# A new order for the head of a hybrid layer: x first, modulation in five groups, seven column units

## What is computed

```python
def reference(x, c, ...):
    c_act = silu(c)
    mod = c_act @ w_mod + b_mod                 # 1024 -> 6 * 1024
    sh_m, sc_m, gt_m, sh_f, sc_f, gt_f = split(mod, 6)
    h = rms_norm(x, g_pre_mix) * (1.0 + sc_m) + sh_m
    y = hybrid_mixer(h, w_in, ...)
    x = x + gt_m * rms_norm(y, g_post_mix)
    h = rms_norm(x, g_pre_mlp) * (1.0 + sc_f) + sh_f
    y = square(relu(h @ w_up)) @ w_down
    return x + gt_f * rms_norm(y, g_post_mlp)

def hybrid_mixer(h, ...):
    b_a, c_a, v_a, x_b, g_b, u_a, u_b = split(h @ w_in, 7)
    y_a = b_a * causal_dwconv(c_a * v_a, conv_a_w, conv_a_b)     # 3 taps
    x_b = causal_dwconv(x_b, conv_b_w, conv_b_b)                 # 4 taps
    r = sigmoid(block_diag(x_b, w_r) + b_r)                      # 8 blocks of 128
    i = sigmoid(block_diag(x_b, w_i) + b_i)
    a = exp(-8 * r * softplus(-lam))
    rec = linear_scan(a, sqrt(1 - a * a) * (i * x_b))
    y_b = rec * gelu(g_b)
    m = sigmoid(u_a) * (y_a @ w_a_out) + sigmoid(u_b) * (y_b @ w_b_out)
    return m @ w_o
```

## Time and profile before

| | |
|---|---|
| Time, median of 3 runs | 849.9 us (848.84 to 850.04) |
| Span of the profiled execution | 846.6 us, from its first to its last instruction |
| Between the span and the median | 3.3 us |
| TensorE matmuls busy | 819.2 us, 97% |
| VectorE | 459.7 us, 54% |
| ScalarE | 379.5 us, 45% |
| GpSimd | 19.8 us, 2% |
| Chain that ended last | TensorE 93%, VectorE 4%, ScalarE 1%, transfers 1% |
| Transfers | 109.42 MB, mean 129 GB/s |

### The profile page before, as it was taken

How to read it: one execution, slowest core, us unless ns; L and a number is a source line. 1 busy time by engine, 2 the same in 40 slices (tenths; PEclk the granted TensorE clock), 3 DMA queues, 4 the chain that set the end, 5 groups by cost and what they waited for, 6 DMA issues and landing times.

```text
span 846.6 us, 10887 instructions
## 1 busy us (share of the span) xinstructions
PE 819.2 (97%) x3714; PEld 682.4 (81%) x3714; DVE 459.7 (54%) x598; ACT 379.5 (45%) x530; POOL 19.8 (2%) x21
## 2 busy tenths in 40 slices
PE   3699999999999999999999999999999999999997
PEld 3578888888888888888888898888888888888885
DVE  5966776666676556555774664333333433333335
ACT  6337777666665444444343653222222322222233
POOL 2311000000000000000000000000000000000000
PEclk9699999999999999999999999999999999999999
DMA  9934333325068666666337034333332223233202
GB/s 306 316 107 107 106 105 105 105 81 180 25 190 237 180 188 197 198 194 178 124 125 224 14 87 125 99 99 99 99 99 90 89 95 100 99 99 99 99 0 99
DMA packets 136438, 109.42 MB, mean 129 GB/s; under 512 B 3925, under 2 KB 120801, under 8 KB 136417
## 3 DMA queue, kind: packets, MB, share of 16 engines
q1 hardware_dynamic: 136192, 109.10, 42.9%
q0 software_dynamic: 160, 0.04, 0.0%
q10 hardware_dynamic: 64, 0.02, 0.0%
HBM read 107.04 MB, written 2.10 MB: 129 GB/s over the span
## 4 chain that ended last, share of the span: by engine, by line
PE 93%; DVE 4%; ACT 1%; DMA 1%; issue 1%; SPq 0%; DVEq 0%; ACTq 0%
PE ps L330 31%; PE ps L331 31%; PE ps L332 31%; DVE mod L837 3%; DMA xs<-in_x_dram 1%; ACT junk L506 1%; PE ps L1265 0%; PE ps L1165 0%; DVE ht_lo L883 0%; DVE k_pos L818 0%; PE ps L1238 0%; PE ps L1237 0%; ACT xnt L531 0%; ACT ht_hi L533 0%; DVE xnt L859 0%
## 5 line engine op out<-in xcount | busy, mean ns | idle before, releaser
L788 DVE TENSOR_TENSOR w_lo<-raw,w_hi 128x1024 fp32r<-128x1024 f32 x131 | 160.2, 1224 | 63.4 <-ACT w_hi L493 56.7
L330 PE MATMUL ps<-ht_hi,w_hi 128*128 128x512 f32 x448 | 177.0, 395 | 3.0 <-DVE ht_lo L883 3.0
L331 PE MATMUL ps<-ht_lo,w_hi 128*128 128x512 f32 x448 | 176.5, 394 | 0.0
L332 PE MATMUL ps<-ht_hi,w_lo 128*128 128x512 f32 x448 | 176.0, 393 | 0.0
L493 ACT ACTIVATE w_hi<-raw 128x1024 fp32r<-128x1024 f32 x132 | 138.3, 1050 | 37.6 <-PE ps L332 31.2
L330 PE MATMUL ps<-h_hi,w_hi 128*128 128x512 f32 (+1 forms) x288 | 105.5, 366 | 0.0
L331 PE MATMUL ps<-h_lo,w_hi 128*128 128x512 f32 (+1 forms) x288 | 105.4, 366 | 0.0
L332 PE MATMUL ps<-h_hi,w_lo 128*128 128x512 f32 (+1 forms) x288 | 105.4, 366 | 0.0
L330 PEld LDWEIGHTS ps<-ht_hi,w_hi 128*128 128x128 f32 x448 | 85.3, 190 | 20.7 <-issue 3.0
L332 PEld LDWEIGHTS ps<-ht_hi,w_lo 128*128 128x128 f32 x448 | 85.3, 190 | 18.0
L330 PE MATMUL ps<-w_hi,hd_hi 128*128 128x512 f32 x256 | 99.7, 390 | 0.0
(11 more groups left out here) (181 smaller groups left out, 1012.3 us busy)
## 6 DMA issues: line engine op xcount, KB each, us to landing
raw<-in_w_in_dram SPq DMA_DIRECT2D x52, 512.0 KB, 4.8
modraw<-in_w_mod_dram SPq DMA_DIRECT2D x32, 512.0 KB, 4.2
raw<-in_w_mlp_up_dram SPq DMA_DIRECT2D x32, 512.0 KB, 4.1
raw<-in_w_mlp_down_dram SPq DMA_DIRECT2D x32, 512.0 KB, 3.3
mod_raw<-in_w_mod_dram SPq DMA_DIRECT2D x16, 512.0 KB, 6.6
xs<-in_x_dram SPq DMA_DIRECT2D x8, 512.0 KB, 6.3
raw<-in_w_a_out_dram SPq DMA_DIRECT2D x8, 512.0 KB, 5.3
raw<-in_w_b_out_dram SPq DMA_DIRECT2D x8, 512.0 KB, 5.7
```

The lines of the kernel that those rows point to most:

```text
L330: nc.tensor.matmul(dst, l_hi, r_hi, start=first, stop=False)
L331: nc.tensor.matmul(dst, l_hi, r_lo, start=False, stop=False)
L332: return nc.tensor.matmul(dst, l_lo, r_hi, start=False, stop=last)
L788: V.tensor_tensor(w_lo[:, slot, :], raw[:, slot, :], f(w_hi[:, slot, :]), ALU.subtract).then_inc(w_lo_ready, 1)
```

## The change

What it does:

- SyncE loads x first. The vectors follow the second tile of x. Then the modulation and the first weights alternate.
- The modulation comes in five groups of channel blocks, (0), (1), (2, 3), (4, 5), (6, 7). Its pieces are 16 chunks of 512 KB (two transfers of 256 KB each), in 8 buffers instead of 3 larger ones. Group 0 is summed by TensorE alone, from the raw chunks, with c_act as the moving operand; the others by VectorE as before, group 1 with 2 x 128 columns to a step.
- Seven column units are summed block by block instead of five: the three first and the three second of XB, C and V, with B of n = 1. The weights come as one transfer of 512 KB to each channel block, with 256 columns of each of B, C, V and XB (those of n = 0 and 1). B of n = 0 (unit 7) is split from the same load and done as a column unit of its own.
- w0_hi and w0_lo are rings of four channel blocks, 896 columns each. w0_lo is made by VectorE, not by GpSimd.
- The softplus steps stand behind the head, not between the steps on mod0.
- TensorE then does unit 7, gates(0), units 8 and 9, gates(1), units 10 and 11, and the loop begins at n = 3. PSUM banks of n = 0 and 1 and of the first gates change; c_sb and the product C x V of n = 1 stand ahead of its convolution.

The diff, cut to its core:

```diff
+    GROUPS = ((0,), (1,), (2, 3), (4, 5), (6, 7))
+    N_FIRST, W0_RING = 7, 4
...
+        FIRST_BANK = ((0, 1, 2, 7), (6, 4, 5, 3))
+        FIRST_DONE = ((1, 2, 3, 8), (4, 5, 6, 7))
+        FIRST_UNITS = ((0, 5, 0), (1, 1, 0), (2, 3, 0), (0, 6, 1), (1, 2, 1), (2, 4, 1), (3, 0, 1))
...
+            def load_mod0(c):
+                g, m, num = CHUNKS[c]
+                if c >= M0_BUFS:
+                    g0, m0, num0 = CHUNKS[c - M0_BUFS]
+                    if g0 == 0:
+                        sp_eng.wait_ge(mod0_sum, 1)
+                    else:
+                        sp_eng.wait_ge(mod0_acc, acc_count(g0, m0 + num0 - 1))
+                ks = GROUPS[g]
                 for a in range(2):
+                    sp_eng.dma_start(chunk_view(c)[:, :, a, :],
+                                     w_mod_v[:, m:m + num, a * D + ks[0] * P:a * D + (ks[-1] + 1) * P]).then_inc(mod0_in[c % M0_BUFS], 16)
...
+            def load_first_units(g):
+                for k in GROUPS[g]:
+                    src = w_in_v[:, k, 0:4 * D].rearrange("p (j n) -> p j n", j=4)
+                    sp_eng.dma_start(raw0[:, k, :].rearrange("p (j n) -> p j n", j=4),
+                                     src[:, :, 0:2 * P]).then_inc(raw0_in[g], 16)
...
-            load_mod0(0)
             for t in range(TB):
                 sp_eng.dma_start(xs[:, t, :], x_v[:, t, :]).then_inc(xr_in[t], 16)
-                if t == 0:
+                if t == 1:
                     load_vectors(sp_eng, vectors[1::3], vec_in)
...
+            load_mod0_group(0)
+            load_first_units(0)
+            load_first_units(1)
+            load_mod0_group(1)
+            load_first_units(2)
+            load_mod0_group(2)
+            load_first_units(3)
+            load_mod0_group(3)
+            load_mod0_group(4)
+            load_first_units(4)
...
-            for q in range(NB // 2):
-                pool.wait_ge(w0_hi_ready, q + 1)
-                nc.gpsimd.tensor_tensor(w0_lo[:, :, cs], raw0[:, :, cs], w0_hi[:, :, cs].bitcast(f32),
-                                        ALU.subtract).then_inc(w0_lo_ready, 1)
...
+            act.wait_ge(xnt_ready, 4)
+            modulate(0, 0)
+            first_units_hi(1)
+            act.wait_ge(xnt_ready_dve, 4)
+            modulate(1, 1)
+            for g in (2, 3):
+                first_units_hi(g)
+                for k in GROUPS[g]:
+                    modulate(k, g)
+            modulate(6, 4)
+            first_units_hi(4)
+            modulate(7, 4)
+            A(w_hi[:, 3, :].rearrange("p (k n) -> p k n", k=NB), raw0[:, :, 0:P], ACT.Copy).then_inc(w_hi_ready, 1)
+            split_hi(2 * RING, 0)
+            act.wait_ge(sp_step, 1)
+            A(sp[:, 1, :], sp[:, 0, :], ACT.Exp).then_inc(sp_act, 1)
...
+            first_units_lo(0)
+            modulation_columns(0)
+            input_lo(0)
+            first_units_lo(1)
+            accumulate(1, range(NB))
+            modulation_columns(1)
+            accumulate(2, range(0, 2))
+            input_lo(1)
+            accumulate(2, range(2, NB))
+            first_units_lo(2)
+            modulation_columns(2)
+            accumulate(3, range(0, 2))
+            input_lo(2)
+            accumulate(3, range(2, 4))
+            input_lo(3)
+            accumulate(3, range(4, NB))
+            first_units_lo(3)
+            modulation_columns(3)
+            accumulate(4, range(0, 2))
+            input_lo(4)
+            accumulate(4, range(2, 4))
+            input_lo(5)
+            accumulate(4, range(4, NB))
+            modulation_columns(4)
+            input_lo(6)
+            first_units_lo(4)
+            input_lo(7)
...
+            split_lo(2 * RING, 0)
+            for i in range(SP_STEPS):
+                softplus_step(i)
...
-            mix(0, lambda: None, (RING + 2, RING + 3, RING + 4, None))
+            mix(0, lambda: None, (9, 10, 11, None))
             recurrence_gates(0)
-            mix(1, lambda: recurrence_scan(0), (None,) + tuple(2 * RING + j for j in range(1, RING)))
+            mix(1, lambda: recurrence_scan(0), (None,) * 4)
...
+            COLUMNS_AT = {(0, 3): 1, (1, 5): 2, (3, 1): 3, (5, 1): 4}
             for k in range(NB):
+                g = next(i for i, ks in enumerate(GROUPS) if k in ks)
+                pe.wait_ge(w0_lo_ready, g + 1)
                 pe.wait_ge(h_lo, k + 1)
+                for i, (j, col, n) in enumerate(FIRST_UNITS):
+                    if (k, i) in COLUMNS_AT:
+                        mod0_columns(COLUMNS_AT[k, i])
...
+            column_unit(N_FIRST, 3, ht_hi, ht_lo, bank(0, 3))
...
+            gates(0)
+            pe.wait_ge(xc_tap, 1)
+            column_unit(8, 0, ht_hi, ht_lo, 0)
+            pe.wait_ge(r_ready, 1)
+            column_unit(9, 1, ht_hi, ht_lo, 1)
+            gates(1)
+            pe.wait_ge(i_ready, 1)
+            column_unit(10, 2, ht_hi, ht_lo, 2)
+            pe.wait_ge(ya_f32, 2)
+            column_unit(11, 3, ht_hi, ht_lo, 3)
+            with pe.Fori(3, NB) as n:
+                mix(n)
```

More of the change, by code:

```diff
@@ L566, in recurrence_root, with mix @@
                 A(q_t[:, :], q_t[:, :], ACT.Sqrt).then_inc(mult_ready, 1)
-            def mix(n, after_xb, splits, xb_bank=0):
-                act.wait_ge(unit_done, 4 * n + 1)
+            def mix(n, after_xb, splits):
+                xb_bank = bank(n, 0)
+                act.wait_ge(unit_done, done(n, 0))
                 wait(act, xc_conv, 3 * n)
@@ L575, in mix @@
                   bias=cols[:, ds(C_BB + n, 1)]).then_inc(xc_tap, 1)
-                first = isinstance(n, int) and n == 0
+                first = isinstance(n, int)
                 if first:
-                    act.wait_ge(unit_done, 2)
-                    A(c_sb[:, :], ps[:, 1, :], ACT.Copy).then_inc(c_copied, 1)
+                    act.wait_ge(unit_done, done(n, 1))
+                    wait(act, cv_ready, n)
+                    A(c_sb[:, :], ps[:, bank(n, 1), :], ACT.Copy).then_inc(c_copied, 1)
                 if splits[0] is not None:
@@ L834, in mod0_steps @@
                         V.tensor_scalar(acc, part, c_act[:, 0:1], None, ALU.mult).then_inc(mod0_acc, 1)
                     else:
[L836 to L841 removed]
+                        dve.wait_ge(mod0_acc, acc_count(g, m - 1))
@@ new lines, in first_units_lo, with input_lo @@
+            def first_units_lo(g):
+                ks = GROUPS[g]
+                slot = ks[0] % W0_RING
+                dve.wait_ge(w0_hi_ready, g + 1)
+                V.tensor_tensor(w0_lo[:, slot:slot + len(ks), :], raw0[:, ks[0]:ks[-1] + 1, P:],
+                                f(w0_hi[:, slot:slot + len(ks), :]), ALU.subtract).then_inc(w0_lo_ready, 1)
+            def input_lo(k):
+                dve.wait_ge(h_hi, k + 1)
+                V.tensor_tensor(ht_lo[:, k, :], xnt[:, k, :], f(ht_hi[:, k, :]), ALU.subtract).then_inc(h_lo, 1)
@@ L914, in mix @@
             def mix(n, after_conv, splits):
-                first = isinstance(n, int) and n == 0
+                first = isinstance(n, int)
                 if first:
-                    dve.wait_ge(unit_done, 3)
-                    dve.wait_ge(c_copied, 1)
-                    V.tensor_tensor(cvp[:, KA - 1:], c_sb[:, :], ps[:, 2, :], ALU.mult).then_inc(cv_ready, 1)
+                    dve.wait_ge(unit_done, done(n, 2))
+                    dve.wait_ge(c_copied, n + 1)
+                    wait(dve, ca_conv, 2 * n)
+                    V.tensor_tensor(cvp[:, KA - 1:], c_sb[:, :], ps[:, bank(n, 2), :], ALU.mult).then_inc(cv_ready, 1)
                 dve.wait_ge(xc_tap, n + 1)
```

283 lines of the change are left out of this document (132 added, 151 removed).

## The result

The changed kernel takes 854.69 us (854.08 to 856.85, 4 runs) against 849.37 us (848.39 to 850.04, 4 runs) of the kernel before, measured together: a ratio of 1.0068, with a 95% interval from 1.0052 to 1.0083. It is 5.3 us slower, by more than a measurement can confuse with no change; the prediction was 849.2 us, with a range that ended at 852.2. The profiled execution of the changed kernel took 854.39 us, its span is 852.6 us: 6.0 more than before.

The account below looks back on a forecast made before the run. VectorE was taken to bound the head, transfers close behind, and matmuls the rest. The head's gain of 4.5 us less 3.8 of new wait gave -0.7: span 845.9, time 849.2 us; 8-in-10 range 845.6 to 852.2.

Parts of the forecast that it names:

- a new wait at gates(1): TensorE behind the head: two units no longer cover the recurrence, a wait of 3.7 us, gates(1) starting at 93.0 us.
- The transposes: Start of the head: x first lets TensorE's transposes end at 15.5 us instead of 17.46.
- The columns of group 0: Start of the head: w0_lo of group 0 1.0 us and its columns 0.3, done at 19.3 us.
- 16 small matmuls, beside VectorE's copies: Group 0 on TensorE: 16 small matmuls instead of VectorE steps, eight of which took 1.87 us at the low clock.
- The string from there: VectorE's steps, subtractions and copies after group 0's columns at 19.3 us, leading to block 6 at 62.0 us.
- The chain between the gates: ScalarE and VectorE from g_lo(0) at 74.6 us to g_lo(1) at 92.9, some 1.1 us added to 17.17.
- The clock behind the wait: Rival: matmuls behind the wait at gates(1), and block 1, run at 1.2 GHz; +2.6 us, 852.5; chance 0.15.
- The rival of the transfers: Rival in the head: smaller modulation pieces transfer slower, at 260 GB/s; +2.8 us, 852.7; chance 0.05.
- the one in which VectorE is not freed: Rival in the head: VectorE's steps stay at 0.97 us although GpSimd's subtractions are gone; +5 us, 855; chance 0.06.
- The quick head: Rival: transposes done at 14.2 us and the clock up ahead of group 1's columns; -2.5 us, 847.4; chance 0.18.
- bounds on x to 16.5 us: Start of the head: transposes could end as late as 16.5 us if the vectors queue behind x.
- nearly cancel: Head, subtractions moved from GpSimd to VectorE: 6 us of VectorE's steps come back against 7.9 us added.

Follow-up runs that it names:

- e5: Changed kernel with 48 and 12 extra small matmuls, results unused, keeping TensorE busy from the start: 860.30 us, ratio to the kernel before 1.0127.
- e1: Changed kernel with group 0 of the modulation summed by VectorE instead of TensorE: 853.03 us, ratio to the kernel before 1.0057.
- e2: Changed kernel with the split of unit 11's weights moved behind the first recurrence: 853.19 us, ratio to the kernel before 1.0056.
- e6: Changed kernel with XB, C and V of n = 0 done first in the last two blocks: 854.38 us, ratio to the kernel before 1.0063.
- e4: Changed kernel with 18 matmuls, results unused, filling the wait ahead of gates(1): 853.45 us, ratio to the kernel before 1.0055.
- e8: Kernel before with only its five subtractions moved from GpSimd to VectorE: 843.70 us, ratio to the kernel before 0.9936.
- e9: Changed kernel with the five w0_lo subtractions made by GpSimd again: 866.86 us, ratio to the kernel before 1.0203.
- e10: Kernel before with subtractions on VectorE, x loaded first and the first four mod steps behind x's tiles: 843.83 us, ratio to the kernel before 0.9940.
- e11: Kernel before with only x loaded first and the first four mod steps behind x's tiles: 849.54 us, ratio to the kernel before 1.0006.
- e3: Changed kernel with TensorE doing unit 10 ahead of gates(1) instead of behind it: 853.18 us, ratio to the kernel before 1.0059.

## Why the prediction was wrong

The form, a new wait at gates(1) that takes back what the head gains, was right, but the head did not gain: its start was priced as VectorE's, and it was TensorE's. Four terms were off, all to the same side. The step that failed is TensorE's work at the start: above all the columns of group 0, which the sum held at nothing beside VectorE's copies, and before them the transposes.

- **The transposes.** Forecast end 15.5 us from VectorE's pace; VectorE's tiles were even earlier (12.8 us), but the 32 transposes took 6.32 us and ended at 16.68. I took the tiles for their pace and let only the last eight, at 5.32/32 us each, follow. In both kernels the transposes run without a gap, 0.21 us apart and then 0.11: 5.32/32 is a mean of these two paces (the two levels of the clock, as e5 shows), and with x early more of them (25) fall into the slow part. +1.2 us.
- **The columns of group 0.** "16 small matmuls, beside VectorE's copies" was wrong in count and price: the profile has 32 instructions (two for each of these products in float32), half of them 0.11 and half 0.21 us apart, 5.36 us, and VectorE waited 2.57 us for them. Its columns were done at 23.05 us instead of 19.3, and what the transposes don't explain of that is 2.6 us. This is the largest of the four; e1 gave 2.65 us of the start and 1.7 us of the time back. Its size is partly chance: the clock fell in the middle of them at 19.2 us, and in executions where it fell later (e2, e6) they took 3.73 us and VectorE waited 0.94. The rows of it were at hand: x8 in the earlier trace rows are four products, as L1165 stands in a loop of two blocks and two halves.
- **The string from there.** It held: steps of 0.52 and 0.78 us, subtractions of 1.08 and 2.02, no step stretched. From those columns to block 6 I forecast 42.7 us and the trace has 42.8; block 6 at 65.84 (forecast 62.0), xbp at 71.67 (67.7), g_lo(0) done at 78.55 (74.6) are all late by the first two terms, 3.8 to 4.0 us.
- **The chain between the gates.** Forecast 18.3 us from g_lo(0) to g_lo(1), measured 19.49. I counted the splits of ScalarE by their durations and missed what they wait for: unit 11's slot is that of unit 7. e2 took 2.1 us out of it (so the rest was 0.9 shorter than I had it), e6 showed it as the second anchor. +1.2 us.
- **The clock behind the wait.** I had it as a rival (1.7 us), with its own row. It came: from gates(1) to gates(2) 19.19 us for 78 matmuls, 1.5 us more than 17.7; e4 got 1.2 us back. Its condition, a wait of about 4 us, was part of the forecast itself, so it belonged in the sum and not beside it. (The same rival put 15 matmuls at half rate at 3.0 us lost; at 0.227 us each it is 3.4.) It is not sure to come: in e2's profiled execution the wait of 2.69 us was followed by no such loss (17.80 us).

Together 4.0 (g_lo(0)) + 1.2 + 1.5 = 6.7 us on a forecast span of 845.9: 852.6, as the trace of this execution has it.

The rival of the transfers did not come (326 to 348 GB/s with pieces of 256 KB), nor did the one in which VectorE is not freed. The quick head did not either: it was the slow one, and I had no case for TensorE setting the start, only bounds on x to 16.5 us.

**The larger misreading** is one that the sum does not show, since it enters as a difference of nearly equal terms. I valued the move of the subtractions at 6 us back against 7.9 us added, "nearly cancel". The 6 us came from the mean of one group of steps (0.972 against 0.76) and left out whatever else stood beside GpSimd, such as the 2.36 us of a step on eight columns. For the five units of the kernel before it is 8.4 against 4.5, and alone it makes that kernel 5.2 us faster (e8). In the changed kernel it is worth 12.2 us (e9). So the whole change is this gain of 5 us and a reordering that costs 11 (854.69 against 843.70). Taken in the other order the reordering costs 17 us (866.86 against 849.57) and the move gives 12 back: the two parts are not independent, but in both orders the reordering is the loss.

What the reordering costs is in the table above: against e8 the first matmul is 1.9 us later, TensorE waits 7.4 us more, and small matmuls and clock take 1.6 us more. It had two aims in the string, and neither was short any more once GpSimd was out of the way. x early gave nothing (e10, e11). Seven units at a time were to fill gaps of TensorE in the head, but in e8 these are 1.7 us in all, while the price is that XB(0) is done at the end of a longer head: xbp at 71.67 us, against 62.69 before, with two units instead of three to cover the recurrence. That last reading rests on e3, where the lateness only moved, on e6 and on the rows; a head like the new one with five units was not tried, and so the split of the 11 us between the groups and the number of units stays open. So does what sets the moments at which the clock rises and falls in the head: in the executions with the same head the fall comes between 18.9 and 21.7 us.

## What to carry to other kernels

Look at what a second engine does to its neighbour's instructions one by one, with all their kinds, ahead of any new order: a step of eight columns that takes 2.36 us says more than a mean. Where several accumulations are run side by side to fill gaps, first count the gaps that would be left without it, and follow the one result on which the serial chain behind hangs: it now comes last. And count the instructions of small float32 products in the trace, not in the source, and ask of each moved split or copy which slot it waits for.
